# The 32x32 products of a block inverse: sixteen small ones against four of full size, in a re-ordered kernel

## The reference

```
state = state * w_t + (state a_t) b_t^T + v_t k_t^T        y_t = state r_t
```

```
inverse = [ X11   X11 A12 X22 ]
          [  0        X22     ]
```

## Time and profile before

| | us |
|---|---|
| median of 3 runs (2266.09 to 2271.28) | 2267.68 |
| the profiled execution, whole | 2262.68 |
| its span | 2260.9 |
| TensorE busy | 2226.6 (98%) |
| its weight loads, beside the products | 1842.1 (81%) |
| VectorE busy | 1540.7 (68%) |
| ScalarE busy | 828.5 (37%) |
| GpSimd busy | 599.9 (27%) |

### The profile page before, as it was taken

One profiled execution on the slowest core, in us unless ns is written; L12 is line 12 of the kernel. 1 busy time (PEld: TensorE's weight loads), 2 busy tenths in 40 slices (PEclk: granted clock), 3 DMA queues, 4 the chain that ended last, 5 costly groups with the idle time before them and its releaser, 6 DMA issues.

```text
span 2260.9 us, 31568 instructions
## 1 busy us (share of the span) xinstructions
PE 2226.6 (98%) x12344; PEld 1842.1 (81%) x12344; DVE 1540.7 (68%) x2562; ACT 828.5 (37%) x1436; POOL 599.9 (27%) x465
## 2 busy tenths in 40 slices
PE   8999999999999999999999999999999999999998
PEld 7888888878787888888888888888888888887877
DVE  5676976768867444565448777763776666678999
ACT  5333234233333433223334454442233333335431
POOL 3212322123103322043123122200022222225552
PEclk9999999999999999999999999999999999999999
DMA  4121221211223334853222112132222222233325
GB/s 154 47 56 43 65 56 41 60 51 56 60 76 123 121 112 146 287 186 125 103 67 51 52 48 56 39 131 103 85 75 84 84 84 84 84 108 120 98 91 176
DMA packets 249316, 208.59 MB, mean 92 GB/s; under 512 B 44624, under 2 KB 218320, under 8 KB 249168
## 3 DMA queue, kind: packets, MB, share of 16 engines
q1 hardware_dynamic: 249168, 206.58, 29.2%
HBM read 152.00 MB, written 47.71 MB: 88 GB/s over the span
## 4 chain that ended last, share of the span: by engine, by line
PE 84%; DVE 9%; DMA 2%; issue 2%; ACT 1%; POOL 1%; SPq 1%; DVEq 0%; ACTq 0%
PE PS L120 81%; PE PS L123 3%; DVE acc L129 1%; DMA wSrcA<-in_w_down_dram 1%; DVE Nn L129 1%; DVE Ntmp L129 1%; DVE wSrcS L129 1%; SPq L146 1%; POOL wLoA L129 1%; DVE wLoS L129 1%; DVE ST L137 1%; DMA Wraw<-in_w_in_dram 0%; DVE ot L129 0%; DVE Zt L129 0%; POOL wLoS L129 0%
## 5 line engine op out<-in xcount | busy, mean ns | idle before, releaser
L120 PE MATMUL PS<-Hhi,Whi 128*128 128x512 f32 (+1 forms) x1304 | 422.7, 391 | 4.3 <-DVE Hlo L129 2.7
L120 PE MATMUL PS<-Hhi,Wlo 128*128 128x512 f32 (+1 forms) x1304 | 421.2, 390 | 0.0
L120 PE MATMUL PS<-Hlo,Whi 128*128 128x512 f32 (+1 forms) x1304 | 421.2, 390 | 0.0
L120 PEld LDWEIGHTS PS<-Hhi,Whi 128*128 128x128 f32 x1304 | 240.6, 190 | 50.8 <-issue 6.3
L120 PEld LDWEIGHTS PS<-Hhi,Wlo 128*128 128x128 f32 x1304 | 242.2, 190 | 45.9 <-issue 1.6
L120 PEld LDWEIGHTS PS<-Hlo,Whi 128*128 128x128 f32 x1304 | 242.1, 190 | 46.0 <-issue 1.4
L126 ACT ACTIVATE Whi<-Wraw 128x512 fp32r<-128x512 f32 x170 | 106.7, 629 | 392.7 <-PE PS L120 388.5
L129 POOL TENSOR_TENSOR Wlo<-Wraw,Whi 128x512 fp32r<-128x512 f32 x82 | 121.2, 1479 | 414.7 <-ACT Whi L126 414.4
L129 DVE TENSOR_TENSOR Ntmp<-Nn 32x30 f32<-32x30 f32 (+14 forms) x240 | 90.3, 376 | 24.3 <-DMA Nn<-scr_ns 17.7
L129 DVE TENSOR_TENSOR Nn<-Nn,Ntmp 32x30 f32<-32x30 f32 (+14 forms) x240 | 93.5, 389 | 6.7
L129 DVE TENSOR_TENSOR Wlo<-Wraw,Whi 128x512 fp32r<-128x512 f32 x88 | 65.0, 742 | 29.2 <-ACT Whi L126 28.3
(11 more groups left out here) (491 smaller groups left out, 5225.5 us busy)
## 6 DMA issues: line engine op xcount, KB each, us to landing
Wraw<-in_w_in_dram SPq DMA_DIRECT2D x126, 256.0 KB, 2.9
scr_g<-stg SPq DMA_DIRECT2D x24, 512.0 KB, 3.1
tg<-scr_g SPq DMA_DIRECT2D x24, 512.0 KB, 3.8
scr_fb<-fb SPq DMA_DIRECT2D x22, 512.0 KB, 4.1
gwA<-in_w_in_dram SPq DMA_DIRECT2D x40, 256.0 KB, 3.4
wA<-in_w_gate_dram SPq DMA_DIRECT2D x38, 256.0 KB, 3.2
wA<-in_w_up_dram SPq DMA_DIRECT2D x38, 256.0 KB, 3.3
wSrcA<-in_w_down_dram SPq DMA_DIRECT2D x48, 192.0 KB, 2.9
```

Of the source, the lines that this page charges most:

```text
L120: return self.h.matmul(out, lhsT, rhs, start=start, stop=stop, skip_group_check=True)
```

## The change

m1 and m2 are done for four matrices at a time. X11t and X22c become tiles of 128 partitions: four matrices stand below each other, and four such groups beside each other. The weights of m1 are taken from a new tile N12 of 128x4x128, zeroed once, with the 32x32 blocks on the diagonal of each 128x128 tile; V1 becomes such a tile too. So each product has a full 128x128 tile of weights and 32 moving columns, and there are four of them for m1 and four for m2, where there were sixteen each.

```diff
@@ tensor_program.stage
-            pe.wait_ge(*S.x11_dma.at(u))
-            for h in range(2):
-                for c in range(8):
-                    q = 8 * h + c
-                    t = pe.mm(bk[0:32, q * 32:(q + 1) * 32], na[0:32, h, c, 32:64], K.X11t[:, q, :])
+            pe.wait_ge(*S.min_dma.at(u))
+            for r in range(4):
+                t = pe.mm(bk[:, r * 32:(r + 1) * 32], K.N12[:, r, :], K.X11t[:, r, :])
...
-            for q in range(16):
-                t = pe.mm(bk[0:32, q * 32:(q + 1) * 32], K.V1[:, q * 32:(q + 1) * 32], K.X22c[:, q, :])
+            pe.wait_ge(*S.init_dve.at("v1"))
+            for r in range(4):
+                t = pe.mm(bk[:, r * 32:(r + 1) * 32], K.V1[:, r, :], K.X22c[:, r, :])
@@ scalar_program.stage
-            act.act(K.V1[:], banks.of(("m1", u))[0:32, :], ACT.Copy)
+            for a in range(0, 128, 32):
+                act.act(K.V1[a:a + 32, :, a:a + 32], banks.of(("m1", u))[a:a + 32, 0:128].rearrange("p (r t) -> p r t", r=4),
...
-            act.act(K.Tt[0:32, :, 32:64], banks.of(("m2", u))[0:32, :].rearrange("p (q t) -> p q t", q=16),
+            for a in range(4):
+                act.act(K.Tt[0:32, 4 * a:4 * a + 4, 32:64], banks.of(("m2", u))[32 * a:32 * a + 32, 0:128].rearrange("p (r t) -> p r t", r=4),
@@ vector_program.init
+        dve.memset(K.N12[:], 0.0).then_inc(*S.init_dve.tick("n12"))
+        yield
+        dve.memset(K.V1[:], 0.0).then_inc(*S.init_dve.tick("v1"))
@@ vector_program.invert
                 dve.wait_ge(*S.xtw_dma.at(u - 1))
-                dve.wait_ge(*S.stage_pe.at(("m2", u - 1)))
@@ sync_program.invert
+            if u:
+                sp.wait_ge(*S.stage_pe.at(("m1", u - 1)))
+            sp.wait_ge(*S.init_dve.at("n12"))
+            for a in range(4):
+                sp.dma(K.N12[32 * a:32 * a + 32, :, 32 * a:32 * a + 32],
+                       na[0:32, a // 2, 4 * (a % 2):4 * (a % 2) + 4, 32:64]).then_inc(*S.min_dma.tick(("n12", u), by=16))
...
-            sp.dma(K.X11t[:], D["scr_xt"][u].rearrange("q (s t) -> s q t", s=32)).then_inc(*S.x11_dma.tick(u, by=16))
-            sp.wait_ge(*S.xsw_dma.at(u))
-            sp.dma(K.X22c[:], xs_v[1]).then_inc(*S.x22_dma.tick(u, by=16))
+            for a in range(4):
+                sp.dma(K.X11t[32 * a:32 * a + 32], xt_v[:, 4 * a:4 * a + 4, :]).then_inc(*S.min_dma.tick(u, by=16))
...
+            for a in range(4):
+                sp.dma(K.X22c[32 * a:32 * a + 32], xs_v[1][:, 4 * a:4 * a + 4, :]).then_inc(*S.x22_dma.tick(u, by=16))
```

More of the change, by code:

```diff
@@ L410, in __init__ @@
         self.Tt = m1("Tt", [64, 16, 64])
-        self.Nn = m1("Nn", [32, 32, 32])
+        both = m1("Nn", [64, 32, 32])
+        self.Nn, self.Nt = both[0:32], both[32:48]
         self.Ntmp = m1("Ntmp", [32, 256])
-        self.X11t = m1("X11t", [32, 16, 32])
-        self.X22c = m1("X22c", [32, 16, 32])
-        self.V1 = m1("V1", [32, 512])
-        self.Nt = at("Nt", [32, 32, 32], F32, offset=m1.at - 4096)
+        self.X11t = m1("X11t", [128, 4, 32])
+        self.X22c = m1("X22c", [128, 4, 32])
+        self.N12 = m1("N12", [128, 4, 128])
+        self.V1 = m1("V1", [128, 4, 128])
+        m1.at += 1024
         self.Xs = [m1(f"Xs{i}", [128, 2, 64]) for i in range(2)]
@@ L1401, in stage @@
             act.wait_ge(*S.stage_pe.at(("m1", u)))
-            act.act(K.V1[:], banks.of(("m1", u))[0:32, :], ACT.Copy).then_inc(*S.stage_act.tick(("m1", u)))
+            act.wait_ge(*S.init_dve.at("v1"))
+            for a in range(0, 128, 32):
+                act.act(K.V1[a:a + 32, :, a:a + 32], banks.of(("m1", u))[a:a + 32, 0:128].rearrange("p (r t) -> p r t", r=4),
+                        ACT.Copy).then_inc(*S.stage_act.tick(("m1", u)))
             yield
@@ new lines @@
+        "d1014o2do2d15odod5o2d8ododo2d10o4",
+    "act":
+        "q2w2awa3q4awaqa3qa8w2ewe2wp2wp3wepwpwes2ws2wfp5w2fpwpw3fws5wfs8wpgwfwgwep4w2es4wps2ps3wes4wgp2wp3gwp"
+        "wfpw2fw2fws5ws8wpwfgwgwep4w2es4wps2ps3wes4wgp2wfp3gwpwfpw4fws5wfs8f2wpwfgwgwep3wpwes3wspsps4wes4wgp2"
+        "wfp3gwfpfwfpw2fw3f3wfs3ws10wf3wgwfgfw2f2w2fs2fs5ws2wf2wgwtSw2tTgStTS4tSTtSTS3t3S2tStS4tSt2S2t2S5t3S2"
+        "t2S5t3S2t2S5t3S2t2S5t3S2t2S5t3S2t2S5t3S2t2S5t3S2t2b3wbwtwt2wtw2bwbwb2w4b2wlwblw2bw5mwm2wmwm3wmwm3wm2"
+        "wm3n3h2n2h2n2h2nh2n2h2n2h2n2h2n2h2r3k2w3v3kw2kwk2wowkwvkv2wx2ryxyxy2zwzoz2x3wy2xwk2ycrwyx4z2wozkr2zr"
+        "2kwy2wvyz2v2zyrwcx2zx2woy4x3wz2xwk2zrzcr2ywyz2yzr2ykzkwx2okxy2xycwykx2wxvz2vzvxrzwy3woz2yz2cwx2wk2xy"
+        "3rxykwk2r2z2rx2zxrxzkwokcy2kywz2yz2xwxvxy2vxvy2rcwx3wxoz4wywydwyrdyrkcwdkdw3i2wdi2wd2i2di2n2h4n2h4nh"
+        "2nh2nh2nh2Sw2uwS2TwTS2uSTS2uTS5u2S2uS4uSuS2uS4uSuS2uS4uSuS2uS4uSuS2uS4uSuS2uS4uSuS2uS4uSuS2uS4uSuS2u"
+        "S4uSuS2uS4uSuS2uS4uSuS2uS4uSuS2uS4uSuS2uS4uSuS2uS4uSuS2uS4uSuS2uS4uSuSuw2uwuwH3SH2SHuS5H7SuSu2H2S4uS"
+        "uSuH5uSuH2S4uSuHSHuH3u2SHuS5u2SuHuSuHS5H3uHSH2SH3S5H2SH2S7H5SHS6HSH5S6H2SH3S5H2SH2S7H5SHS6HSH5S5HS21",
@@ new lines @@
+    "dve":
+        "Zq2a4q2aqaqa4qa2qa2j3a2j3e2p2spep9i2ei2es2i7pi11pipi7pi9fipfpfp3ip3ipfi26f2i2pi14s2is2i3s2ci2s3ci3sc"
+        "i4cisi2ci4ci3cpipcg2ig2ifgigfifigi3gi10ei6pep8sps5cs3ci2ce2i2cscsc2i3pcgcgig2i3gigi2pipgfi3pi4gi6pip"
+        "ip3ip3fpfi36fif2i3pi12fis4i4s2ci2s3ci3sci4cisi2ci3ci4picpicg2ig2ifgfgi6gi7gi2ei6pep8sps5cs3ci2ce2i2c"
+        "scsc2i3pcgcgig2i3gigi2pipgi3pi7gi5pipip3fp3fpfi11fi25f2i2pi12s2ifs2fs2fcis4ci4cisi2ci5ci4ci2ci5cpgpg"
+        "ig2ifgfgi6gi8giei8pep8sps5cs3ci2ce2i2cscsc2i3pcgcgig2i3gigi2pipgifpif2ififgi2pipip3ip3ipfifi16fif2if"
+        "2ififi22fifif5pf2ififi4s2is2i4s2ci3s2csi3sci4sci4ci4cifcficg2ig2igigi5gi2fgi2fi19f2w2f2s4ws2cs2c4wcf"
+        "cfcg2Twg2TgwTSgTwTgTwgT2STS2TS2TST3S2uS2u3S2uSuS4u2S2uSu2S4uS2u2Su2S4uS2u2Su2S4uS2u2Su2S4uS2u2Su2S4u"
+        "S2u2Su2S4uS2u2Su2S4uS2u2Su2b2uwbuwbuwuwtwtwbtwbtwbtwbtwbtwtwb3wtlbwtbltwbtwbtwtwtwtwtwtmtwtmwt3wmt2m"
+        "wt2wmt2mwt2mwtmn4hnhn2hnhn2hnhnh2n3h2n3h2n3h2n3h2r5w3k3wkwk3wk5wkwok2wokx2r2wxy2ryxrxr4yxyz2r2zr2yr2"
+        "wrzrzr2x3y2zxowyxor2wryxr2yvx2wxkxyxz3xkwzr2kzkrzr4y2owykz2woyzyr2z2r3yr2wrvx3r3zr2xrxr2y2ryrxwy2x3o"
+        "yz2xzxowr3wxzr2zkzkr2vy2kyrz2r2zwr2y2z2ykzx3kwy2xyx2y2kovx2wxyz2ozxk2wxr2z2xr6zwr6y2ryr3z2yzywyz3ovx"
+        "2wxoy2rwr2xyr2kxy2kxykr2kwz2kzrx2r2xzr2zkx3zwk2vy3koz2yzywkokzyzr2x3ywyzxyxy2xr4vx2rwrxyx2r3z2r2zr2w"
+        "xr3z3owy2oyrwr4ydwydr2ydvkwd2k2dw3A2wdAdAwd3A2dA2n3hnhnh2n2hnh3n2h2n2h2n2h2n2h2T3STSwSTw2S3wuTuT2SuT"
+        "3uT2S3TS3u3Su6S3uS3u2Su6S3uS3u2Su6S3uS3u2Su6S3uS3u2Su6S3uS3u2Su6S3uS3u2Su6S3uS3u2Su6S3uS3u2Su6S3uS3u"
+        "2Su6S3uS3u2Su6S3uS3u2Su6S3uS3u2Su6S3uS3u2Su6S3uS3u2Su6S3uS3u2Su6S3uS3u2Su6S3uS3u2Su8wuwu2wu3wuH3SHS2"
+        "HSHSHS2uH5SHuHS2HSuSH2S2u2H4SH2S2HSHSu2S2uH4SH2S2uSHSu2S3HS2uSHSHuS2uHuH2uHuHSHuS2HSHSu2S2uHuHuHuHuS"
+        "uHS2HSuSu2S2H2u3HuSH2S2uSHSu2S2u2Hu3HuSH2S2uSuSHuS2H2u3Hu2H2Su2S2HSHSu2S2HuH2uHuSuHS2HSuSu2S2H2u3HuS"
+        "H2S2uSHSu2S2u2Hu3HuSH2S2uSuSHuS2H2u3Hu2Hu6SuS2BSBSBS2Bu7SuS2uSuSuS2uB2u3B2u3SuS2uSuSuS2uB2uB2u9B4",
@@ L3178 @@
[L3178 to L3179 removed]
+    "0123010123012301230010110100101010110100110001010101011010101010011001010101010110101010100101101010"
+    "1010101001010101011001101010101010100101010101101001100101010101101010101010011001010101010110101010"
+    "1001010110101010100101010101010110100110010101011010067523401675234016752340167523401675234016752340"
@@ new lines @@
+    "1671010101010101010101010102102101011010010210110011020102110012102102102102102010201201120102102102"
+    "0120012012011021021012010120012012010211012012012012012010201021020120112012012012012001021021020110"
+    "2102102101201201020120120120120102110210120120120020102101120120120011201201010010110120100110120145"
+    "6701234567012345670123456701234567012345670123456701234567012345670123456701234567012345670122034526"
+    "7013452670134526701345267013452670134526701345267013452670130122301345270202013220130160132"
```

92 lines of the change are left out of this document (31 added, 61 removed).

## The result

The changed kernel takes 2248.95 us (median of 6 runs, 2243.45 to 2253.95), the kernel before 2267.24 us beside it: a ratio of 0.9913, 95% interval 0.9894 to 0.9933. Run once more it took 2249.47 us against 2265.76, ratio 0.9923 (0.9903 to 0.9943). So it gains 16 to 20 us, where 11.1 were forecast.

What follows compares the result with a forecast made beforehand. The prediction took TensorE, busy for 98% of the span, as the bound. Its terms summed to -11.1 us, from a median of 2267.7 to 2256.6 us, with a range of 2248.5 to 2267.

Steps and rivals of the forecast that it cites:

- the clock's term: Recurrent branch: all five falls of the granted clock to 0.50 go, 1.4 us each, -7.0 us.
- m1, G, m2: Eight units: m1 and m2 at 1.01 us each, G alone 1.61, against 3.69 together; -1.2 us.
- c0, c1 apart, five units: Units 1, 2, 3, 5, 6: dense steps between c0 and c1 cost 2.74 us against 2.25; +2.5 us.
- stall between c0 and c1: Units 1, 3, 5: the second c gets its own bank, so 1.55 us each goes; -4.65 us.
- gn7, and gn6 and gn0: Only gn7 was priced: five dense steps later, its 1.85 us wait for VectorE goes; -1.8 us.
- ks, kt: Shorter waits at ks2 and ks4, now ten steps further behind their operands; -1 us.
- waits for m1's tiles: Later landings of X11t, issued in four transfers, make m1 wait; +1.5 us over all units, ends 0 and 20.
- rest of the order: Changed numbers of returns and part-size runs, with unseen waits of the new order; +0.5 us, bounds -3 and +6.
- Rival 1: Clock falls as often as now, since full tiles with 32 columns leave TensorE idle; 2263.6 us, chance 0.13.
- rival 3: New waits in attention or unit 7, for a bank or VectorE result, eat 8 us; 2264.6 us, chance 0.14.
- so nothing there: SyncE: ten more transfers a unit, 3.2 us of issue in some 70, cost its queue nothing.
- Rival 2: m1 waits for its tiles, four X11t landings behind N12's four, 2.5 us a unit; 2275 us, chance 0.08.

Runs made afterwards that it cites:

- The run with more returns: Kernel before with 16 pairs of adjoining n steps, behind the recurrent branch, each parted by one dense step; 2275.61 us.
- own banks: Kernel before with c0 in G's bank and c1 in m2's in units 1, 3 and 5, the bo step behind c1; 2259.82 us, ratio 0.9972.
- unit 7 apart: Kernel before with only unit 7's order changed: bo7 six dense steps earlier, mix4 and mix5 three; 2277.86 us.
- the products in the old order: Changed kernel's four full products for m1 and m2 each, in the order strings and bank picks of before; 2282.1 us, ratio 1.0071.

## Why the prediction was right and wrong

The direction, the bound, the stall and most of the clock's term were right. The step that failed is the price of the part-size steps around m1 and m2, and with it three terms that no row stood for: unit 7, gn6 and the waits for m1's tiles. The sum was 5.4 us short in the recurrent branch, and that it was no further off is luck in part: 8.2 us of error one way stand against 3.3 the other. The terms, from the loads of both profiles between the 150th and 2200th dense load:

| term, us | forecast | measured |
|---|---|---|
| m1, G, m2 | -1.2 | -4.0 |
| c0, c1 apart, five units | +2.5 | +1.8 |
| stall between c0 and c1 | -4.65 | -4.65 |
| clock | -7.0 | -7.6 |
| gn7, and gn6 and gn0 | -1.8 | +0.3 |
| ks, kt | -1 | -0.8 |
| unit 7 (bo7, mixes, A7.1) | 0 | -2.6 |
| waits for m1's tiles | +1.5 | 0 |
| rest of the order (y and de +1.2, one c1 +0.3) | +0.5 | +1.5 |
| sum | -11.1 | -16.0 (of -16.5) |

(gn7 alone gave 1.6 and gn6 took 1.7.)

**m1 and m2** is the step that failed most. The durations were right: eight full records take 1.01 us, with 32 columns as with 2 or 128, and the rule of the Trainium skill on the columns of a weight load holds ("TensorE: Matmul & The Clock Gate", "LDWEIGHTS (loading the stationary operand)"). Wrong was "G loses its neighbours of part size ... entering costs 0.36 and leaving 0.17, as c shows: 1.61 alone". Those are c's prices, with the dense stream's 512 columns before it and its own 128 behind. Behind m1 G's entry is 0.04, and it leaves with 0.07. In the forecast's own measure G alone is 0.36 + (132.91 - 131.84) = 1.43, and m1 with G 190.81 - 188.60 = 2.21, where 1.01 + 1.61 - 0.12 = 2.50 was forecast. That makes 3.23 in six units and 3.46 in two against 3.69, so -3.2 and not -1.2. The rest is the 0.12 for each return: with 0.106 given back by the next pair the run costs 3.54 us before (3.65 - 0.11), and after 2.21 + 1.01 - 0.21 = 3.01 in six units and 3.11 in two, where G alone is 1.40 - 0.11: 6 x 0.53 + 2 x 0.43 = 4.0. The run with more returns shows that second price by itself; the first is read from the traces.

**c0 and c1 apart** is off by the price of a return: 2.68 - 2.21 - 0.11 = 0.36 each. The stall of 1.55 us and its three places were exact.

**The clock**: all five falls went, in both executions, and cost 1.5 each (4.0 us between the dense loads of the five stretches and 3.6 in their side steps). By the mean granted clocks, 0.9967 in six executions against 0.9932 in the 17 beside them, after has about 16 us less at half speed, which at that price is an estimate of 7 us. But one reason was wrong. Taking away the hole between the c's leaves the mean clock where it was (own banks); taking m2 away from G raises it. Rival 1, falls as often as before with full tiles of 32 columns, did not come true in the new order. What remains there, in some executions, are falls behind waits of 1.1 to 3.0 us at c1 or a y step; behind a wait of 1.17 us in the second execution of after there is none.

**gn**: gn7's 1.85 us went as forecast, but the term looked at gn7 alone: gn6, which stood 26 dense steps behind y6.7 and stands 18, now waits itself:

```profile
606.59 0.42 PEld L123 LDWEIGHTS PS<-cst,Yt 128*128 128x128 f32 x4 [1.92 <-issue]
```

**Unit 7** was named as "several us of waits" in rival 3, as a place to lose, and stands in the sum at nothing. It was a place to gain: bo7, the two mixes and A7.1 stood 6.5 us in one run before and take 2.6 less apart. TensorE's order alone does not give this (unit 7 apart); that it is VectorE's order that does is likely and was not run by itself.

**m1's tiles**: the 1.5 us for late landings had no row that showed a wait, and none came.

**SyncE**: "so nothing there" was right for this kernel and wrong as a reason. The ten transfers are on the way of the next Nn and cost up to 2.2 us of its time; m1 did not come to wait, and that goes with the more dense steps which the new order leaves units 1, 3, 5 and 7 from their last A step to m1 (93 to 96, where they were 77 to 90); no run shows this by itself. Something did come of it at de10 of unit 0, which waits 0.65 and 1.39 us in the two profiles of after and 0.15 and 0.44 in those of before. Rival 2 (2275) saw the danger at m1's tiles, of which not one was late in after (in the old order one stood, 0.86 us); its size was that of the products in the old order, by other waits and by the clock.

The rest of the difference to the medians (16 to 18 us there against 16.5) is within a measurement.

## What to carry to other kernels

Price a return or an entry over the whole neighbourhood, from the last undisturbed load before it to the first undisturbed one behind, since the next step may give back what the first one lost. A change of form that looks neutral on its own engine can be worth only what its order makes of it: here it cost 16 us in one and gave 4 in the other, by a queue of transfer issues, a row of small copies and more falls of the clock. Before a wait between two engines is called the price of an edit, look at the granted clock of the same stretch. And take a fall of the clock or a wait for a transfer from two executions before it is called a property of the kernel.
